# A two-block transformer kernel on one core: values and gates by token, rotation halves by ScalarE

## What is computed

```python
IN_SIZES = [NSA_Q_DIM, NSA_KV_DIM, NSA_KV_DIM, NSA_KV_DIM, NSA_KV_DIM, NSA_KV_DIM, NSA_KV_DIM,
            NSA_GATE_DIM, RET_QK_WIDTH, RET_QK_WIDTH, RET_V_WIDTH, RET_V_WIDTH]
def rope(x, pos):
    ...
    x1, x2 = xf[..., :half], xf[..., half:]
    return jnp.concatenate([x1 * cos - x2 * sin, x2 * cos + x1 * sin], axis=-1).astype(x.dtype)
def first_block(...):
        xn = rms_norm(h, ln1_w[l])
        proj = xn @ w_in[l]
        (nq_, nkc, nvc, nks, nvs, nkw, nvw, ngate,
         rq, rk, rv, rg) = jnp.split(proj, split_points, axis=-1)
        o_nsa = nsa_mixer(...)
        o_ret = retention_mixer(rq, rk, rv, rg, ret_norm_w[l])
        mix = jnp.concatenate([o_nsa, o_ret], axis=-1)
        h = h + mix @ w_out[l]
```

## Time and profile before

| | us |
|---|---|
| median of 3 runs | 1512.98 (1509.92 to 1514.96) |
| profiled execution | 1510.54 |
| its span, first to last instruction | 1508.80 |
| PE busy | 1440.4 (95%) |
| DVE busy | 888.6 (59%) |
| POOL busy | 681.2 (45%) |
| ACT busy | 565.2 (37%) |

### The profile page before, as it was taken

The page is one execution under the profiler, slowest core; times in us unless marked ns, Lnnn a source line. Parts: engine busy times, 40 slices in busy tenths (PEclk is TensorE's granted clock), DMA queues, the critical chain, the costliest instruction groups (busy, mean ns, idle before and its releaser), DMA issues.

```text
span 1508.8 us, 19162 instructions
## 1 busy us (share of the span) xinstructions
PE 1440.4 (95%) x7100; PEld 1156.4 (77%) x7100; DVE 888.6 (59%) x1447; ACT 565.2 (37%) x743; POOL 681.2 (45%) x516
## 2 busy tenths in 40 slices
PE   5999999999999999998899999989988999999997
PEld 4777766778888887886788788768867888888886
DVE  4783667557757788976592555335675323432357
ACT  5332467443222121225343655543335331332231
POOL 2441255526455555653461434445533454454553
PEclk9999999999999999999999999999998999999999
DMA  8322130026646454232835433253304233223222
GB/s 316 100 70 103 57 112 2 29 84 216 242 165 228 159 192 163 84 112 98 134 136 140 150 137 133 98 196 134 112 33 154 86 109 110 86 84 112 84 86 82
DMA packets 50693, 185.86 MB, mean 123 GB/s; under 512 B 15088, under 2 KB 16496, under 8 KB 35888
## 3 DMA queue, kind: packets, MB, share of 16 engines
q1 hardware_dynamic: 30672, 165.68, 31.5%
q10 hardware_dynamic: 19936, 19.02, 5.0%
HBM read 169.86 MB, written 12.59 MB: 121 GB/s over the span
## 4 chain that ended last, share of the span: by engine, by line
issue 32%; PE 25%; POOL 24%; DVE 3%; ACT 0%; POOLq 0%; DVEq 0%
POOL wlo L1533 23%; PE bank L454 5%; PE bank L455 5%; PE bank L456 5%; PE bank L504 3%; PE bank L506 3%; PE bank L505 3%; PE bank L692 1%; DVE Alo L1651 1%; DVE X L2409 0%; PE bank L478 0%; PE bank L763 0%; DVE Ahi L1649 0%; DVE X L2421 0%; POOL wlo L1541 0%
## 5 line engine op out<-in xcount | busy, mean ns | idle before, releaser
L1533 POOL TENSOR_TENSOR wlo<-raw,whi 128x512 fp32r<-128x512 f32 x440 | 633.1, 1470 | 761.4 <-ACT whi L997 761.4
L454 PE MATMUL bank<-Ahi,whi 128*128 128x512 f32 x1080 | 432.4, 400 | 17.8 <-DVE Alo L1651 4.7
L456 PE MATMUL bank<-Ahi,wlo 128*128 128x512 f32 x1080 | 422.8, 392 | 0.0
L455 PE MATMUL bank<-Alo,whi 128*128 128x512 f32 x1080 | 422.6, 391 | 0.0
L997 ACT ACTIVATE whi<-raw 128x2048 fp32r<-128x2048 f32 x112 | 214.6, 1916 | 234.8 <-PE bank L506 212.6
L454 PEld LDWEIGHTS bank<-Ahi,whi 128*128 128x128 f32 x1080 | 204.1, 189 | 68.8 <-issue 9.3
L455 PEld LDWEIGHTS bank<-Alo,whi 128*128 128x128 f32 x1080 | 204.2, 189 | 43.4 <-issue 2.4
L456 PEld LDWEIGHTS bank<-Ahi,wlo 128*128 128x128 f32 x1080 | 203.8, 189 | 43.2
L504 PE MATMUL bank<-whi,Bhi 128*128 128x512 f32 x496 | 193.2, 390 | 1.7 <-DVEq L1884 1.7
L506 PE MATMUL bank<-whi,Blo 128*128 128x512 f32 x496 | 193.0, 389 | 0.0
L505 PE MATMUL bank<-wlo,Bhi 128*128 128x512 f32 x496 | 193.0, 389 | 0.0
(11 more groups left out here) (399 smaller groups left out, 1848.2 us busy)
## 6 DMA issues: line engine op xcount, KB each, us to landing
raw<-in_ws SPq DMA_DIRECT2D x112, 1024.0 KB, 5.0
adaw<-in_ada SPq DMA_DIRECT2D x48, 512.0 KB, 4.7
spill<-stage ACTq DMA_DIRECT2D x32, 256.0 KB, 2.2
X<-in_x SPq DMA_DIRECT2D x8, 512.0 KB, 6.7
gates<-spill SPq DMA_DIRECT2D x16, 256.0 KB, 5.5
w1k<-in_w1k SPq DMA_DIRECT2D x1, 2048.0 KB, 16.3
w1v<-in_w1v SPq DMA_DIRECT2D x1, 2048.0 KB, 20.7
XM<-spill ACTq DMA_DIRECT2D x8, 256.0 KB, 3.3
```

The source lines that it names most:

```text
L454: pe.matmul(ps[:], wh, hi[:, k], start=(k == 0), stop=False)
L455: pe.matmul(ps[:], wh, lo[:, k], start=False, stop=False)
L456: ins = pe.matmul(ps[:], wl, hi[:, k], start=False, stop=(k == kn - 1))
L1533: pool.tensor_tensor(wlo[slot][:, part], raw[slot][:, part], rd(whi[slot][:, part]), ALU.subtract).then_inc(sem("lo_split"), 1)
```

## The change

1. vs, vw and the gates are computed in one block `va`, by token: a 128-token slice of the input is stationary and 280 weight columns stream (128 + 128 + 24), into four banks (one for each slice). The heads' values are the block `rv` with 512 columns. Both run in the `STAGGERED` order. The seven turns go, and ACT copies the banks straight to `VT`, `GT` and `RV`. The sigmoid is taken later, once, on all gates.
2. The product with `rot` goes. ACT copies four groups of 32 partitions from `F4` to `Fb` with the halves exchanged (`halves_turned`), the sign sits in the sine table, and DVE multiplies `Fb` in place.
3. The sequence of the stage is kc, vc, va, q0 to q3, ks, kw, rq0, rk0, rq1, rk1, rv, rg0 to rg3. The compressed branch moves forward with its keys, retention behind `rv`. `retention_turn(2)` and `retention_out(2)` move behind attention.
4. The copies of compressed keys and values into `kc2` and `vc2` are issued by SP instead of ACT, and w1v behind tile 3.

The number of tiles is the same, 12 for the stage.

```diff
-WIN = (["kc", "vc", "q0", "q1", "q2", "q3", "ks", "kw", "vs", "vw", "gate",
-       "rq0", "rk0", "rv0", "rq1", "rk1", "rv1", "rg0", "rv2", "rg1", "rv3", "rg2", "rg3"])
+WIN = ["kc", "vc", "q0", "q1", "q2", "q3", "ks", "kw", "rq0", "rk0", "rq1", "rk1", "rg0", "rg1", "rg2", "rg3"]
+VALUES = {"va": (3, 280, [[0, 1, 2, 3, 4], [5, 6, 7]]), "rv": (4, 512, [[0, 1, 2, 3], [4, 5, 6, 7]])}
+STAGGERED = ((0, 0), (0, 1), (0, 2), (1, 0), (0, 3), (1, 1), (1, 2), (1, 3))
...
-            def post2(n, c):
-                if n in ROPED:
-                    pe.wait_ge(sem("rope_in"), T.due("rope_in"))
-                    ps, where = bank("T")
-                    done(pe.matmul(ps[:], c_("rot"), F4[c % 4][:], start=True, stop=True), f"rot_{n}", where)
+            def value_runs(name):
+
+                per, cols, split = VALUES[name]
+                g = INDEX[f"{name}.0"]
+                outs = [bank("G"), bank("G"), bank("O"), bank("O")]
+
+                def run(q, i):
+                    ks = split[q]
+                    for k in ks:
...
+                        pe.matmul(ps, h, wh, start=(k == 0), stop=False)
+                        pe.matmul(ps, h, wl, start=False, stop=False)
+                        ins = pe.matmul(ps, l, wh, start=False, stop=(k == DC - 1))
...
+            for c in range(2, 12):
+                gemm(WIN[c], Ahi, Alo)
+                sum_squares(WIN[c - 1])
+                if c == 4:
                     hidden()
-                elif c == 14:
+                elif c == 6:
                     hidden_turn(0)
                     hidden_turn(1)
-                elif c == 15:
+                elif c == 7:
                     compressed_keys()
-                elif c == 16:
+                elif c == 8:
                     compressed_values()
...
+                if c >= 8:
+                    compressed_scores(c - 8)
+                if c >= 10:
+                    compressed_turn(c - 10)
+            run = value_runs("rv")
+            for x, (q, i) in enumerate(STAGGERED):
+                run(q, i)
+                if x == 1:
+                    retention_scores(0, (0, 1))
+                elif x == 2:
+                    compressed_turn(2)
+                elif x == 3:
+                    retention_scores(0, (2, 3))
+                elif x == 4:
+                    compressed_turn(3)
...
+            def halves_turned(n):
+
+                if n not in ROPED:
+                    return
+                r = ROPED.index(n)
+                act.wait_ge(sem("rope_in"), r + 1)
+                if r >= 2:
+                    act.wait_ge(sem("roped"), r - 1)
+                for b in range(4):
+                    to, fr = 32 * b, 32 * (b ^ 1)
+                    ins = act.activation(Fb[r % 2][to:to + 32], F4[r % 4][fr:fr + 32], ACT.Copy)
+                ins.then_inc(sem("rot_ready"), 1)
...
                 tt(o, f[:], rope[:, 0], ALU.mult).then_inc(sem("dve_step"), 1)
-                dve.wait_ge(sem("dve_step"), v.did("dve_step"))
-                tt(Fb[0][:], ps[:], rope[:, 1], ALU.mult).then_inc(taken(f"rot_{n}")[0], 1)
-                dve.wait_ge(*taken(f"rot_{n}"))
-                tt(o, o, Fb[0][:], ALU.add).then_inc(sem("roped"), 1)
+                dve.wait_ge(sem("rot_ready"), r + 1)
+                tt(turned_[:], turned_[:], rope[:, 1], ALU.mult).then_inc(sem("dve_step"), 1)
+                v.did("dve_step")
+                dve.wait_ge(sem("dve_step"), v.did("dve_step"))
+                tt(o, o, turned_[:], ALU.add).then_inc(sem("roped"), 1)
...
+            sp.dma_start(w1[0][:], d["w1k"].rearrange("p (a b) -> p a b", a=16)).then_inc(sem("w1_in"), 16)
+            tiles(2, 3)
             sp.wait_ge(sem("norm_rows"), L.due("norm_rows", NT))
             sp.dma_start(rope[:], d["rope"].rearrange("p (a b) -> p a b", a=2)).then_inc(sem("rope_tab"), 16)
+            tiles(3, 4)
+            sp.dma_start(w1[1][:], d["w1v"].rearrange("p (a b) -> p a b", a=16)).then_inc(sem("w1_in"), 16)
+            sp.wait_ge(*taken("vc"))
+            sp.wait_ge(sem("roped"), 1)
...
-            tiles(2, 10)
+            tiles(4, 7)
```

More of the change, by code:

```diff
@@ L675, in retention_turn @@
                 pe.wait_ge(sem("yn_ready"), T.due("yn_ready"))
-                last = h == RET_H - 1
-                turn(f"mixT{4 + h}", [YN[int(last)][:, i, :] for i in range(NT)], "G" if last else "T")
-            def retention_step(c):
-                for h, b in enumerate(RET_AT):
-                    if c == b + 1:
-                        retention_values(h)
-                    elif c == b + 3 and h < RET_H - 1:
-                        retention_turn(h)
+                turn(f"mixT{4 + h}", [YN[int(h == RET_H - 1)][:, i, :] for i in range(NT)], "T" if h < 2 else "G")
             def scores(u):
@@ new lines, in _ @@
+            for x, (q, i) in enumerate(STAGGERED):
+                run(q, i)
+                if x == 1:
[6 more added lines that the diff above has]
+                    compressed_turn(3)
+            for c in range(12, 16):
+                ps, where = bank("G")
+                if c == 12:
+                    blocks_of(ps, WIN[c], Ahi, Alo, range(4))
+                    retention_values(0)
+                elif c == 13:
+                    blocks_of(ps, WIN[c], Ahi, Alo, range(2))
+                    retention_scores(1, (0, 1))
+                    blocks_of(ps, WIN[c], Ahi, Alo, range(2, 4))
+                elif c == 14:
+                    blocks_of(ps, WIN[c], Ahi, Alo, range(4))
+                    retention_turn(0)
+                else:
+                    blocks_of(ps, WIN[c], Ahi, Alo, range(4))
+                    retention_turn(1)
+                    retention_values(3)
+                    for u in range(AHEAD):
+                        scores(u)
+                if c == 13:
+                    blocks_of(ps, WIN[c], Ahi, Alo, range(4, 6))
+                    retention_scores(1, (2, 3))
+                    done(blocks_of(ps, WIN[c], Ahi, Alo, range(6, 8)), WIN[c], where)
+                else:
+                    done(blocks_of(ps, WIN[c], Ahi, Alo, range(4, 8)), WIN[c], where)
+                if c == 12:
+                    retention_values(1)
+                elif c == 14:
+                    retention_values(2)
@@ L2632, in of @@
         head, _, rest_ = name.partition(".")
-        if name in ("kc", "vc", "ks", "kw", "vs", "vw"):
+        if head in VALUES:
+            out_ = []
+            for k in VALUES[head][2][int(rest_)]:
+                rows = slice(k * P, (k + 1) * P)
+                if head == "va":
+                    out_ += [part["vs"][rows], part["vw"][rows],
+                             np.concatenate([part["gate"][rows], np.zeros((P, P - 24), np.float32)], 1)]
+                else:
+                    out_ += [part["rv"][rows, h * P:(h + 1) * P] for h in range(RET_H)]
+            out_ += [np.zeros((P, P), np.float32)] * (TILE_BLOCKS - len(out_))
+            return np.concatenate(out_, 0)
+        if name in ("kc", "vc", "ks", "kw"):
             return part[name]
```

301 lines of the change are left out of this document (140 added, 161 removed).

## The result

The changed kernel takes 1524.41 us in the median of four runs (1524.10 to 1526.40), the kernel before 1512.85 beside it (1509.92 to 1514.96). The ratio is 1.0081, 95% interval 1.0062 to 1.0100: slower by 11.6 us, where 1510.5 was forecast. The profiled execution after took 1524.62, with a span of 1522.8.

What follows compares the result with a forecast made beforehand. TensorE was taken as the bound. Without new waits the first scores came some 20 us earlier; walked with waits summing to 18 us and 2.0 for the clock, 2.5 us earlier: 1510.5 us, range 1498 to 1520.

Steps and rivals of the forecast that it cites:

- What leaves PE: First stage on TensorE: rotation products 9.5 us, turns 3.2, narrower value and gate products 3.9; sum 16.6 us less work.
- the 3.2 us of the turns: On TensorE: six value turns at 0.44 us and a smaller one for the gates go, 3.2 us.
- Rival 2: Value blocks: a 280-column product costs what a 512-column one does, 21.9 us instead of 12.5; total 1519, chance 0.10.
- Step (a): Stage start to q0's start at 49.2: tile 4 there at about 57, hidden because q2 wants it at 61.
- Step (b): q0 to the hidden rows' copy: rows ready at 105 to 107, PE wants them at 101; wait about 5 us.
- GpSimd's 30% of the stretch: GpSimd busy in 30% of the stretch, so each turn was taken near its lower end, 8.2 us.
- Step (c): From 106 to 151.5: three turns of 8.2 us, PE losing about 5 us there and 8 us behind them.
- the ring: Three new turns at the compressed scores through ScalarE, VectorE and PE; 7.8 to 9.5 us each, 8.2 taken.
- Step (d): From 151.5 to the first scores: PE is the bound again and reaches them at 200.5.
- clock term: 2.0 us added behind the wait of 8 us, for PE at the lower clock level after it.
- Rival 3: Half copies cost 1.1 us each: 2.3 us more per rotation, six on the chain, 14 us; total 1524, chance 0.08.
- Rival 1: PE's waits, 18 us in sum, are half as long and the clock loss is gone: 1499.5, chance 0.25.

Runs made afterwards that it cites:

- tile4_early: ct_late with tile 4 ahead of w1v and the eight small copies on SyncE's queue; 1516.05 us.
- ct_late: The changed kernel with the turns of the third and fourth compressed probabilities and the second four retention scores three value runs later; 1517.39 us.
- rot_back: The changed kernel with the halves exchanged by a PE product with rot again, value blocks and sequence kept; 1519.21 us.
- rot_tile4: rot_back with tile 4 ahead of w1v and the small copies on SyncE's queue; 1510.04 us.
- filled: ct_late with idle PE products, results overwritten, put into its two remaining waits (28 and 19 products); 1513.12 us.
- best_1: rot_back with tile 4 early, kc's exchange one value run earlier, and retention scores and probability turns two or three runs later; 1505.91 us.

## Why the prediction was wrong, by its steps

**What leaves PE** was right in the term that had no row. A value product starts 0.13 us behind the last one, as taken (the 3.2 us of the turns no run takes by itself):

```profile
33.70 0.29 PE L586 MATMUL bank<-whi,Ahi 128*128 128x280 f32 x1
33.83 0.29 PE L587 MATMUL bank<-wlo,Ahi 128*128 128x280 f32 x1
```

The trace has 128 ns. That is nearer to the columns' share, 125, than to the 119 ns that come out, as an estimate, of the Trainium skill's formula for an isolated gap (TensorE: Matmul & The Clock Gate, Back-to-back issue gap). Rival 2 falls with it.

**Step (a)** had tile 4 at 57, and ACT split it at 57.37. It failed in who wants it first. I followed PE's use (q2) and not ACT's queue, where q0's square stands behind the split. PE waited 1.5 us at 60.3.

```profile
57.37 1.92 ACT L1018 ACTIVATE whi<-raw 128x2048 fp32r<-128x2048 f32 x1 [10.14 <-DMA raw<-in_ws]
...
60.30 1.13 PE L568 MATMUL bank<-SQ,con 128*128 128x512 f32 x2 [1.48 <-ACT F L1189]
```

In the changed kernel that moved the chain by 1.6 us (tile4_early against ct_late); in rot_back, where PE waited 5.0 us for it, it cost 6.9 us of stage (rot_tile4). It is hidden in the trace's times by the start, which was 1.4 us earlier.

**Step (b)** had the wait and a wrong end, 110.2 for 106; counted from the pair kc, vc it is 5.6 us late, of which 1.6 are tile 4's. The term that failed is DVE under the split: at most 0.4 was charged for a sine product, 1.06 came, and the cosine product, the sum and the small copy were stretched beside it, 3.8 us in all. The earlier trace rows show the means of these steps, not what one pass beneath a split costs. I also took GpSimd's 30% of the stretch as if it were a chance. It isn't: GpSimd starts when ACT has rounded a tile, which on this chain puts it beside the DVE steps that follow, at 102.9, 131.96 and 155.3.

**Step (c)** named the ring, its order and its three turns, and the wait of 8.5 behind it. Its sizes failed: 31.9 us for 27.5 from first to last exp. Of the 4.4 the half clock made 2.1 (shown by filled, on ct_late, whose first turn is as long), and the dearer copies 1.3 (three times 0.45). The other 1.0 is a difference: ACT waited for PE 1.3 us at full clock too (filled), DVE's two stretched steps added 1.5, and the remaining steps were shorter than taken. The prediction charged the clock behind the last wait only, and took PE's share of a turn at full speed. Behind the ring another 3.9 us. There the walk followed the wrong engine: it had DVE's sine product wait for ACT's second set of copies, which ended at 157.76, and DVE came to it at 159.89, late by its own last pass of 1.37, 1.63 and 1.75 us and a small step of 1.13 for 0.17, again under a split. Of the two sets of copies only the first, 0.45, was on the chain.

**Step (d)** was right to a microsecond, 49.95 us for 49.0. Its clock term was 2.0, and PE stood at 0.50 from 163.24 to 169.0, which is 2.9 us of work. (The terms that it lists add to 46.4 us, where its end has 46.8.)

The sum: 3.5 us up to the first exp, 4.4 in the ring, 3.9 behind it and 0.9 in (d) are 12.7, the distance from 200.5 to 213.19. With the 1.4 us by which this trace's stage began earlier, the first term is 4.9 and the sum 14.1; the medians, 1524.41 for 1510.5, say 13.9. Nearly every term was taken near its lower end, on one chain where nothing averages out. **Rival 3** came to 1524 and so to the measured time by luck, through a copy of 1.1 us; it is 0.63. **Rival 1** had the waits half as long as 18 us; they came to 20.7.

The largest thing is not a size. I held that the waits were the price of a gain of 16.6 us. best_1 shows that most of the price was in three places that have nothing to do with values by token: the exchange on ACT, a tile behind small copies, and scores issued before banks were free. With these mended the stage is 4 to 5 us shorter than before, with 7.1 us less PE work by the prediction's count (3.2 + 3.9). What the value blocks and the new sequence are worth each by itself stays open: no run has one without the other.

## What to carry to other kernels

Moving work from the full engine to a half idle one pays only where it isn't waited for: ask what stands ahead of it in that engine's queue, and who waits behind. A step that reads a bank instead of a second SBUF tile is worth keeping on a chain that runs beside GpSimd. A chain through three engines is to be costed at each step's worst neighbour, and a wait of TensorE at its length plus the half clock behind it, whenever the next wait hangs on PE's work.

## What the runs showed of the hardware

- A ScalarE copy of 32 partitions by 512 from SBUF to SBUF costs 0.63 us, as much as one of 128 partitions (632 ns), and four in a row don't overlap; written to a bank, four take 2.40 instead of 2.55.
- PE worked at 0.50 for 6.8 us behind a wait of 1.8 us (best_1), and for 7.7, 5.0 and 5.8 us behind waits of 7.2, 5.0 and 8.5 us (after): the losses, 3.4, 3.8, 2.5 and 2.9 us of work, don't grow with the wait. Waits of 1.8 to 1.9 us passed without a fall elsewhere (before at 333, ct_late at 154). Seven idle products of 0.23 us kept the clock at 1.00.
- The rest of the kernel, which no edit touches, varies by 3.9 us over the sixteen traces, by 3.1 between the two of after and by 1.1 between the two of before. The clock fell in different places in them. How much of the 3.9 us the clock makes no run shows.
